# Prompt queries of the second mixer in blocks by residue modulo 4

## The chip, the cores and the metric

The kernel runs as one program on one core of a Trainium2 chip. The metric is the device time of one execution in microseconds. One "layer" of a decoder is computed for 256 prompt tokens and 64 sample tokens (8 sequences of 8), all in float32 accuracy.

## The reference, cut to what matters

The input is projected to queries, keys, values and gates; two attention mixers follow, then a gated merge, a layer norm and an MLP. The second mixer (B) has three groups g of 8 heads. Query t of group g reads the keys t - j*dilation for j = 0..127:

```python
B_PATTERNS = ((128, 1), (512, 4), (2048, 16))     # (window, dilation)
for g, (win, dil) in enumerate(B_PATTERNS):
    o, lse = banded_window_attn(qb[:, :, g, :, None, :], kb[:, :, g], vb[:, :, g], dil)
...
w = jax.nn.softmax(jnp.stack(lses, 0), axis=0)     # the three groups are merged by their softmax sums
o = jnp.sum(w[..., None] * jnp.stack(outs, 0), axis=0)
```

With 256 prompt tokens, dilation 4 lets a query see only keys of its own residue modulo 4, at most 64 of them, and dilation 16 at most 16. The first mixer (A) has 16 query heads on 2 key heads, a window of 128, no dilation, and a sink.

## The kernel before, in words

Activations are held with features on partitions and tokens along the free dimension: 256 prompt tokens and 64 sample tokens, 320 columns. Weights come in chunks of 512 rows by 256 columns (`raw`, a ring of 4). ScalarE rounds a chunk to `whi`, VectorE computes the rest `wlo`, and TensorE multiplies a chunk in 24 matmuls of 320 columns: high by high, high by low, low by high (`chunk`, lines 1202 to 1204). Four chunks make a group of 256 output features in one of two PSUM tensors `psM[0]`, `psM[1]`.

**Projections.** Groups 0 to 3 are A's queries, 4 to 9 B's queries (two per dilation group), 10 A's keys and values, 11 to 16 B's keys, 17 to 22 B's values, 23 to 38 the gates. For queries and keys ScalarE copies swapped halves to `rot` (L532) and VectorE applies the rotation in three instructions (L862, L863, L866), the last one writing `qT` for queries and the staging tile `tT` for keys, and counting up `evac`, which TensorE waits for before it writes that PSUM tensor again two groups later. GpSimd copies B's keys from `tT` to `kTb` (L347). TensorE transposes keys and values (`turn`), and ScalarE copies them out (`turn_out`) and stores them from its own queue to a scratch in DRAM, values also to `vnat` (tokens on partitions, two blocks of 128). `kv_stored` counts the stores. GpSimd waits for all of them, then copies prompt and sample keys and values to the outputs, then loads the cached keys of the first sample sequence.

**Attention under the gates.** The 16 gate groups run as 64 chunks. From group 2 on, the steps of attention are laid between the chunks in an order written out by hand: in each of four rounds j there are 12 units (`UNITS`), unit ("B", e, qb) being head e of pair j in query block qb (128 tokens), for all three dilation groups at once. Per step TensorE issues the scores of the unit two ahead, the values of the one before, and the transposes (turn) of the probabilities of the current one, then a chunk. VectorE scales and masks the scores into `S`, takes the maximum (`front`), later normalizes (`back`); ScalarE computes the exponentials (`exps`) and copies turned probabilities from PSUM to `PT` (`turned_probs`).

A B unit of qb 0 meets keys 0..127 in each group: both heads' scores are issued together, heads alternating, three products of 128 columns each (L1255). A B unit of qb 1 meets 256 keys in each group: each head issues its three products of 256 columns in its own step (L1261). So a unit has 384 or 768 score columns, 3 or 6 turned blocks and, for the pair, 6 or 12 value products (L1314).

Units SB and SA are the samples; their cached keys go to `kvbuf` by GpSimd's loads, new keys are added by GpSimd (`add_new_keys`). At the end the attention output `oT` is split in three parts to `ohi` (ScalarE, L661) and `olo` (VectorE, L960), which the branch projections read.

## Time and profile before

| | |
|---|---|
| median of 3 runs | 1818.94 us (1817.2 to 1819.33) |
| profiled execution | 1818.74 us, span 1817.2 us |
| busy TensorE | 1785.7 us, 98% of the span |
| busy VectorE | 970.0 us, 53% |
| busy ScalarE | 783.7 us, 43% |
| busy GpSimd | 128.9 us, 7% |
| DMA | 369.40 MB, mean 203 GB/s |
| granted TensorE clock | 0.996 of full on the mean |

The span is the time from the first to the last recorded instruction of the profiled execution; the time of that execution is 1.5 us longer. "Busy" is the time in which at least one instruction of the engine is in flight. Matmul records overlap, so the distance between two starts is shorter than the duration of one. A matmul of plain fp32 operands leaves two records, a transpose and a matmul of the split operands one.

### The profile page before, as it was taken

To read this page: it belongs to the slowest core of one execution; us is meant where nothing else is said; L and a number is where in the kernel's file an instruction comes from. 1 tells how busy PE (TensorE), PEld (TensorE's weight loads), DVE (VectorE), ACT (ScalarE), POOL (GpSimd) and SP (SyncE) were. 2 spreads that over 40 slices of the span, in tenths; PEclk is the share of its full clock that TensorE was granted. 3 is DMA by queue.
4 is the path that set the end of the run, shared out by engine and by line. 5 is a ranking of instruction groups with operands and counts; after the bars stand their busy time and mean duration, and the time that the engine had idled before them with its cause. 6 is when DMAs were issued, how large, how long until landed. Compare 5 with 4: busy or idle time off the path is not lost.

```text
span 1817.2 us, 34353 instructions
## 1 busy us (share of the span) xinstructions
PE 1785.7 (98%) x13170; PEld 1753.8 (97%) x13170; DVE 970.0 (53%) x1324; ACT 783.7 (43%) x1109; POOL 128.9 (7%) x251
## 2 busy tenths in 40 slices
PE   7999999999999999999999999999999999999996
PEld 7999999988899899999999999999999999999995
DVE  5555453356665655656767444654446544465465
ACT  5444553455665563334445333443334433344333
POOL 4000000021121110100000000000000000000001
PEclk9999999999999999999999999999999999999998
DMA  8555555587777666655565766657666575656742
GB/s 259 148 150 151 165 169 161 164 316 240 254 244 264 221 240 204 210 163 171 184 208 199 233 222 205 208 187 244 202 224 208 187 245 189 236 187 212 240 149 70
DMA packets 272229, 369.40 MB, mean 203 GB/s; under 512 B 13088, under 2 KB 265952, under 8 KB 269200
## 3 DMA queue, kind: packets, MB, share of 16 engines
q1 hardware_dynamic: 252496, 251.58, 45.0%
q0 software_dynamic: 10368, 107.12, 15.3%
q10 hardware_dynamic: 9280, 9.51, 1.5%
q8 instruction: 61, 1.00, 0.2%
q14 instruction: 24, 0.20, 0.0%
HBM read 356.02 MB, written 70.71 MB: 235 GB/s over the span
## 4 chain that ended last, share of the span: by engine, by line
PE 97%; DMA 1%; DVE 1%; ACT 0%; issue 0%; ACTq 0%; SPq 0%; DVEq 0%
PE psM L1202 30%; PE psM L1203 30%; PE psM L1204 30%; DMA s_raw<-in_w_in_dram 1%; PE psT L1288 1%; PE psM L1276 1%; PE psO L1333 1%; PE psM L1261 1%; PE psO L1314 0%; PE psT L1222 0%; PE psO L1323 0%; PE psM L1265 0%; PE psT L1293 0%; DVE s_r L1186 0%; DMA s_xraw<-in_xT_dram 0%; PE psO L1403 0%
## 5 line engine op out<-in xcount | busy, mean ns | idle before, releaser
L799 DVE TENSOR_TENSOR s_wlo<-s_raw,s_whi 128x1024 fp32r<-128x1024 f32 x468 | 570.0, 1225 | 620.2 <-ACT s_whi L475 615.4
L475 ACT ACTIVATE s_whi<-s_raw 128x1024 fp32r<-128x1024 f32 x468 | 491.2, 1057 | 775.2 <-PE psM L1204 750.0
L1202 PE MATMUL psM<-s_xhi,s_whi 128*128 128x320 f32 x1248 | 392.3, 314 | 9.8 <-DVE s_xlo L804 9.8
L1204 PE MATMUL psM<-s_xhi,s_wlo 128*128 128x320 f32 x1248 | 386.6, 310 | 0.0
L1203 PE MATMUL psM<-s_xlo,s_whi 128*128 128x320 f32 x1248 | 386.6, 310 | 0.0
L1203 PE MATMUL psM<-s_glo,s_whi 128*128 128x322 f32 x1024 | 319.5, 312 | 0.0
L1202 PE MATMUL psM<-s_ghi,s_whi 128*128 128x322 f32 x1024 | 318.7, 311 | 0.0
L1204 PE MATMUL psM<-s_ghi,s_wlo 128*128 128x322 f32 x1024 | 318.5, 311 | 0.0
L1202 PE MATMUL psM<-s_uhi,s_whi 128*128 128x320 f32 x1024 | 316.9, 309 | 0.0
L1204 PE MATMUL psM<-s_uhi,s_wlo 128*128 128x320 f32 x1024 | 316.4, 309 | 0.0
L1203 PE MATMUL psM<-s_ulo,s_whi 128*128 128x320 f32 x1024 | 316.4, 309 | 0.0
L1202 PEld LDWEIGHTS psM<-s_xhi,s_whi 128*128 128x128 f32 x1248 | 235.5, 189 | 10.5 <-DVE s_xlo L804 9.8
L1203 PEld LDWEIGHTS psM<-s_xlo,s_whi 128*128 128x128 f32 x1248 | 235.6, 189 | 0.0
L1204 PEld LDWEIGHTS psM<-s_xhi,s_wlo 128*128 128x128 f32 x1248 | 235.3, 189 | 0.0
L1204 PEld LDWEIGHTS psM<-s_ghi,s_wlo 128*128 128x128 f32 x1024 | 194.1, 190 | 0.0
L1202 PEld LDWEIGHTS psM<-s_ghi,s_whi 128*128 128x128 f32 x1024 | 193.4, 189 | 0.1
L1203 PEld LDWEIGHTS psM<-s_glo,s_whi 128*128 128x128 f32 x1024 | 193.3, 189 | 0.1
L1202 PEld LDWEIGHTS psM<-s_uhi,s_whi 128*128 128x128 f32 x1024 | 192.2, 188 | 0.2
L1203 PEld LDWEIGHTS psM<-s_ulo,s_whi 128*128 128x128 f32 x1024 | 192.2, 188 | 0.2
L1204 PEld LDWEIGHTS psM<-s_uhi,s_wlo 128*128 128x128 f32 x1024 | 192.2, 188 | 0.0
L456 POOL DMA_DIRECT2D out_b_s_dram<-in_cache_b_kv_dram x56 | 27.3, 487 | 763.6 <-DVE s_wlo L799 750.7
L1202 PE MATMUL psM<-s_mhi,s_whi 128*128 128x320 f32 x256 | 79.3, 310 | 0.0
(206 smaller groups left out, 1688.0 us busy)
## 6 DMA issues: line engine op xcount, KB each, us to landing
s_raw<-in_w_ff_dram SPq DMA_DIRECT2D x256, 512.0 KB, 3.9
s_raw<-in_w_in_dram SPq DMA_DIRECT2D x156, 512.0 KB, 4.1
s_kvbuf<-in_kT_b_dram POOLq DMA_DIRECT2D x8, 2448.0 KB, 9.2
s_kvbuf<-in_v_b_dram POOLq DMA_DIRECT2D x8, 2304.0 KB, 8.4
s_raw<-in_w_out_dram SPq DMA_DIRECT2D x32, 512.0 KB, 3.6
out_b_s_dram<-in_cache_b_kv_dram POOLq DMA_DIRECT2D x16, 1008.0 KB, 6.6
s_raw<-in_w_branch_a_dram SPq DMA_DIRECT2D x16, 512.0 KB, 3.6
gates_scratch<-s_gstage ACTq DMA_DIRECT2D x16, 320.0 KB, 3.9
```

The costliest lines, as they stand in the source:

```text
L456: pool.dma_start(dst, src).then_inc(out_cache, 16)
L475: act.activation(whi[:, slot], raw[:, slot], ACT.Copy).then_inc(hi_done, 1)
L799: dve.tensor_tensor(wlo[:, slot], raw[:, slot], whi[:, slot].bitcast(F32), ALU.subtract).then_inc(lo_done, 1)
L1202: pe.matmul(out, wh, xh, start=first and k == 0, stop=False)
L1203: pe.matmul(out, wh, xl, start=False, stop=False)
L1204: mm = pe.matmul(out, wl, xh, start=False, stop=last and k == KT - 1)
L1261: mm = pe.matmul(ps[:, g, 0:nk], qTb[64 * e:64 * e + 64, 4 * g + j, qs], kTb[64 * e:64 * e + 64, 4 * g + j, 0:nk], start=True, stop=True)
L1276: mm = pe.matmul(ps[rows, g, 0:KN], Qz[:, g - 1, c, rows], kcache[:, pr, 4 * g - 3 + c], start=c == 0, stop=c == 3)
L1288: mm = pe.transpose(psTf[:, t * P:t * P + P], Sp[:, t * P:t * P + P], ident[:])
L1333: pe.matmul(out[32 * pr:32 * pr + 16, 0:P], PTz[:, 256 * (g - 1) + 64 * c + 16 * pr:256 * (g - 1) + 64 * c + 16 * pr + 16], vcache[:, 4 * ...
```

## The change

Prompt tokens of B are ordered by residue modulo 4: position r*64 + a holds token 4a + r. A query block of 128 then holds two residues: block 0 residues 0 and 1, block 1 residues 2 and 3.

- Groups of dilation 4 and 16 keep queries (`qT`), keys (`kTb`) and values (`vnat`) in this order, so a query block meets only the 128 keys of its own two residues. Group 0 (dilation 1) has its queries in this order and its keys and values in order of tokens: both of its blocks meet all 256 keys.
- Every B unit has 256 + 128 + 128 = 512 score columns, 4 turned blocks and, for the pair, 8 value products. Both blocks issue the scores of both heads at once.
- Reordering is done by instructions that exist already, each split in two, one for the prompt's columns with a step of four elements on one side and one for the samples' columns: VectorE's last rotation addition for B's queries, GpSimd's copy of keys (groups 13 to 16), ScalarE's copy of values (groups 19 to 22), and the third part of the split of `oT`.
- Values of these groups are stored to the scratch in three DMAs in place of two. `kv_stored` goes to 16 stores per counter.
- The masks become four tables of 256 columns: SP loads the first, GpSimd blanks the others with one memset and fills them by 12 loads.
- In the projections the loop over queries starts two groups later (groups 2 and 3 stand before it) and the loop over values is unrolled.

```diff
-            [("S", [P, 3, 768], F32), ("PT", [P, 2, 768], F32), ...
+            [("S", [P, 3, 512], F32), ("PT", [P, 2, 640], F32), ...
-        mask_p = sb("mask_p", [P, 3, 256])
+        mask_p = sb("mask_p", [P, 4, 256])
...
+        def by_residue(ap):
+            return ap.rearrange("p t (r a) -> p t a r", r=4)
+        def in_order(ap):
+            return ap.rearrange("p t (a r) -> p t a r", r=4)
...
+            nc.gpsimd.memset(mask_p[:, 1:4], NEG).then_inc(masks_blank, 1)
...
+            for r2 in range(2):
+                for h in range(2):
+                    early, late = 64 * r2, 64 * r2 + 32
+                    pool.dma_start(mask_p[early:early + 32, 1 + h, 0:P], rows[:, h, r2, 0, P:2 * P]).then_inc(mask_in, 16)
+                    pool.dma_start(mask_p[late:late + 32, 1 + h], rows[:, h, r2, 0]).then_inc(mask_in, 16)
+                for g in range(2):
+                    first = P * g + 64 * r2
+                    pool.dma_start(mask_p[64 * r2:64 * r2 + 64, 3, first:first + 64], a["mask_p"][0:64, g, P:P + 64]).then_inc(mask_in, 16)
...  # GpSimd, keys of groups 13 to 16
+                    pool.tensor_copy(by_residue(kTb[:, to, 0:SEQ]), in_order(tT[:, c % 2, :, 0:SEQ]))
+                    pool.tensor_copy(kTb[:, to, SEQ:NTOK], tT[:, c % 2, :, SEQ:NTOK]).then_inc(kcopy, 1)
...  # ScalarE, store of values of groups 19 to 22
+                        for r2 in range(2):
+                            act.dma_start(rows[:, :, r2], vnat[64 * r2:64 * r2 + 64, 0:2, bass.ds((g - G_V) * GW + P, GW)]
+                                          ).then_inc(kv_stored[par], 16)
+                        act.dma_start(kvn_d[SEQ:NTOK, bass.ds(dcol, GW)], v_to[1]).then_inc(kv_stored[par], 16)
...  # ScalarE, values of groups 19 to 22 from PSUM
+                        act.activation(by_residue(tT[:, par, :, 0:SEQ]), in_order(ps[:, :, 0:SEQ]), ACT.Copy)
+                        act.activation(tT[:, par, :, SEQ:NTOK], ps[:, :, SEQ:NTOK], ACT.Copy).then_inc(evac[par], 1)
...  # VectorE, B's queries
+                if kind == "qb":
+                    out = qT[:, bass.ds(g * 2, 2)]
+                    dve.tensor_tensor(by_residue(out[:, :, 0:SEQ]), in_order(dst[:, :, 0:SEQ]), in_order(rot[:, :, 0:SEQ]), ALU.add)
+                    dve.tensor_tensor(out[:, :, SEQ:NTOK], dst[:, :, SEQ:NTOK], rot[:, :, SEQ:NTOK], ALU.add).then_inc(evac[par], 1)
...  # VectorE, mask of a B unit
-                    nh, n = 1, 3 * nk
+                    nh, n = 1, 512
+                    last = dve.scalar_tensor_tensor(halves(Sp[:, 0:n]), halves(psM[0][:, e, 0:n]), SCALE, mask_p[:, 1 + qb:4:2 - qb], ALU.mult, ALU.add)
...  # ScalarE, third part of the output's split; VectorE's is split alike
+                act.activation(in_order(ohi[:, 8:12, 0:SEQ]), by_residue(oT[:, 8:12, 0:SEQ]), ACT.Copy)
+                act.activation(ohi[:, 8:12, SEQ:NTOK], oT[:, 8:12, SEQ:NTOK], ACT.Copy).then_inc(o_hi, 1)
...  # TensorE, scores
-                if (kind, e, qb) == ("B", 1, 0):
+                if kind == "B" and e == 1:
                     return
...
-                if kind == "B" and qb == 0:
-                    for g in range(3):
+                if kind == "B":
+                    for g, first, keys in ((0, 0, slice(0, SEQ)), (1, SEQ, qs), (2, SEQ + P, qs)):
                         for h in range(2):
                             half = slice(64 * h, 64 * h + 64)
-                            mm = pe.matmul(psM[0][:, h, P * g:P * g + P], qTb[half, 4 * g + j, qs], kTb[half, 4 * g + j, 0:P], start=True, stop=True)
+                            mm = pe.matmul(psM[0][:, h, first:first + keys.stop - keys.start], qTb[half, 4 * g + j, qs], kTb[half, 4 * g + j, keys],
+                                           start=True, stop=True)
...
-                elif kind == "B":
-                    for g in range(3):
-                        mm = pe.matmul(ps[:, g, 0:nk], qTb[64 * e:64 * e + 64, 4 * g + j, qs],
-                                       kTb[64 * e:64 * e + 64, 4 * g + j, 0:nk], start=True, stop=True)
...  # TensorE, turns and values
-                    for t in range((3 if kind == "B" else 2) * (qb + 1)):
+                    for t in range(4 if kind == "B" else 2 * (qb + 1)):
...
-                    for t in range(nb):
-                        g, kb = divmod(t, qb + 1)
+                    for t, (g, kb) in enumerate(((0, 0), (0, 1), (1, qb), (2, qb))):
```

## Rows read from the trace of the kernel before

**Rows 1.** The page: busy us, share and instructions; the chain that ended last.
```profile
PE 1785.7 (98%) x13170; PEld 1753.8 (97%) x13170; DVE 970.0 (53%) x1324; ACT 783.7 (43%) x1109; POOL 128.9 (7%) x251
...
PE 97%; DMA 1%; DVE 1%; ACT 0%; issue 0%; ACTq 0%; SPq 0%; DVEq 0%
```

**Rows 2.** TensorE's waits, whole span: us in total, times, longest us.
```profile
PE psM L1202 <- DVE s_xlo L804: 9.8, 1, 9.8
PE psT L1288 <- ACT s_PT L569: 2.4, 1, 2.4
```

**Rows 3.** Timeline, TensorE, scores: start us, us of the group, engine, line, count.
```profile
448.52 0.94 PE L1255 MATMUL psM<-s_kTb,s_qT 64*128 64x128 f32 x12
449.39 0.66 PE L1323 MATMUL psO<-s_PT,s_vnat 128*64 128x128 f32 x8
...
411.64 1.56 PE L1261 MATMUL psM<-s_kTb,s_qT 64*128 64x256 f32 x6
413.12 0.66 PE L1323 MATMUL psO<-s_PT,s_vnat 128*64 128x128 f32 x8
...
425.65 0.49 PE L1265 MATMUL psM<-s_kTa,s_qT 64*128 64x128 f32 x4
426.08 0.33 PE L1349 MATMUL psO<-s_ident,s_PT 128*128 128x128 f32 x1
...
431.30 0.70 PE L1265 MATMUL psM<-s_kTa,s_qT 64*128 64x256 f32 x4
431.93 0.87 PE L1288 MATMUL psT<-s_ident,s_S 128*128 128x128 f32 x6
```

**Rows 4.** Timeline, TensorE: a group of turns and two groups of values.
```profile
466.39 0.55 PE L1288 MATMUL psT<-s_ident,s_S 128*128 128x128 f32 x3
...
438.48 1.53 PE L1314 MATMUL psO<-s_PT,s_vnat 128*64 128x128 f32 x24
...
472.62 0.88 PE L1314 MATMUL psO<-s_PT,s_vnat 128*64 128x128 f32 x12
```

**Rows 5.** Groups by line and shape: count, busy us, mean ns, idle before.
```profile
L1288 PE MATMUL psT<-s_ident,s_S 128*128 128x128 f32 x120 | 20.1, 287 | 2.4 <-ACT s_PT L569 2.4
...
L1314 PE MATMUL psO<-s_PT,s_vnat 128*64 128x128 f32 x144 | 9.6, 278 | 0.0
...
L824 DVE COPY s_QbS<-s_qT 64x32 f32<-64x32 f32 x48 | 8.8, 184 | 0.5
```

**Rows 6.** Timeline, ScalarE's and GpSimd's, before the first units; idle before in brackets.
```profile
363.55 0.61 ACTq L494 DMA_DIRECT2D kv_scratch<-s_vst  x1
...
367.09 0.58 POOL L362 DMA_DIRECT2D out_a_p_dram<-kv_scratch  x1 [104.34 <-DMA kv_scratch<-s_vst]
...
394.47 1.06 ACT L475 ACTIVATE s_whi<-s_raw 128x1024 fp32r<-128x1024 f32 x1 [5.33 <-DMA s_raw<-in_w_in_dram]
```

**Rows 7.** Timeline, projections: the last rope instruction, and TensorE's next group.
```profile
202.19 0.82 DVE L866 TENSOR_TENSOR s_tT<-s_tT,s_rot 128x640 f32<-128x640 f32 x1
...
211.55 0.39 PE L1202 MATMUL psM<-s_xhi,s_whi 128*128 128x320 f32 x1
```

**Rows 8.** Instructions of one tile: ns min/median/max, first and last start us.
```profile
L347 POOL COPY s_kTb<-s_tT x6: 718/720/724, 188.3 to 262.0; 128x640 f32 x4, 128x640 f32<-128x640 f32 x2
...
L1202 PE MATMUL psM<-s_ohi,s_whi x192: 309/309/410, 685.6 to 770.8; 128*128 128x320 f32 x192
...
L960 DVE TENSOR_TENSOR s_olo<-s_qT,s_ohi x3: 1484/1485/1492, 674.9 to 677.7; 128x1280 fp32r<-128x1280 f32 x3
```

**Rows 9.** Timeline: GpSimd done with new keys, TensorE's scores of SB; round 0 and tightest.
```profile
433.87 0.54 POOL L382 DMA_DIRECT2D s_vca<-in_cache_a_kv_dram  x1
...
436.25 0.44 PE L1271 MATMUL psM<-s_kvbuf,s_QbS 128*32 128x136 f32 x8
...
540.58 0.54 POOL L382 DMA_DIRECT2D s_vca<-in_cache_a_kv_dram  x1
...
540.78 0.44 PE L1271 MATMUL psM<-s_kvbuf,s_QbS 128*32 128x136 f32 x8
```

More of the change, by code:

```diff
@@ L196, in projections @@
             step(1, 0, 1, "q", None)
-            with eng.Fori(0, 4) as i:
-                for c in range(2, 4):
-                    step(i * 2 + c, i, c, "q", None)
+            step(2, 0, 2, "q", None)
+            step(3, 0, 3, "q", None)
+            with eng.Fori(0, 3) as i:
+                for c in range(4, 6):
+                    step(i * 2 + c, i, c, "qb", None)
             step(10, 0, 10, "kva", None)
@@ L206, in projections @@
             step(17, 0, 17, "v", "k")
-            with eng.Fori(0, 2) as i:
-                for c in range(18, 20):
-                    step(i * 2 + c, i, c, "v", "v")
-            step(22, 0, 22, "v", "v")
+            step(18, 0, 18, "v", "v")
+            step(19, 0, 19, "w", "v")
+            for c in range(20, 23):
+                step(c, 0, c, "w", "w")
+        def by_residue(ap):
+            return ap.rearrange("p t (r a) -> p t a r", r=4)
+        def in_order(ap):
+            return ap.rearrange("p t (a r) -> p t a r", r=4)
         def gate_bank(n):
@@ L341, in _, with kcopy_step @@
                     pool.dma_start(dst[32 * pr + 16:32 * pr + 32, 0:3], a[name][16:32, 0:3]).then_inc(mask_in, 16)
[L343 to L357 removed]
+            pool.wait_ge(masks_blank, 1)
+            rows = a["mask_p"].rearrange("(a h r) g n -> a h r g n", h=2, r=2)
+            for r2 in range(2):
[6 more added lines that the diff above has]
+                    pool.dma_start(mask_p[64 * r2:64 * r2 + 64, 3, first:first + 64], a["mask_p"][0:64, g, P:P + 64]).then_inc(mask_in, 16)
+            def kcopy_step(g, i, c, kind):
+                pool.wait_ge(evac[c % 2], i + (c // 2 + 1))
+                to = bass.ds((g - G_K) * 2, 2)
+                if kind == "k":
+                    pool.tensor_copy(kTb[:, to], tT[:, c % 2]).then_inc(kcopy, 1)
+                else:
+                    pool.tensor_copy(by_residue(kTb[:, to, 0:SEQ]), in_order(tT[:, c % 2, :, 0:SEQ]))
+                    pool.tensor_copy(kTb[:, to, SEQ:NTOK], tT[:, c % 2, :, SEQ:NTOK]).then_inc(kcopy, 1)
+            kcopy_step(11, 0, 11, "k")
+            kcopy_step(12, 0, 12, "k")
+            with pool.Fori(0, 2) as i:
+                for c in range(13, 15):
+                    kcopy_step(i * 2 + c, i, c, "by residue")
+            pool.wait_ge(kv_stored[0], 16 * 16)
+            pool.wait_ge(kv_stored[1], 16 * 16)
             kv_rows = kvn_d.rearrange("t (s c) -> t s c", s=2)
@@ L516, in turn_out @@
                     act.wait_ge(turned_out, g - 9)
-                    store(*v_to, (g - G_V) * GW + (KVW + P), GW)
+                    dcol = (g - G_V) * GW + (KVW + P)
+                    if kind == "v":
+                        store(*v_to, dcol, GW)
+                    else:
+                        rows = kvn_d[0:SEQ, bass.ds(dcol, GW)].rearrange("(a h r) n -> a h r n", h=2, r=2)
+                        for r2 in range(2):
+                            act.dma_start(rows[:, :, r2], vnat[64 * r2:64 * r2 + 64, 0:2, bass.ds((g - G_V) * GW + P, GW)]
+                                          ).then_inc(kv_stored[par], 16)
+                        act.dma_start(kvn_d[SEQ:NTOK, bass.ds(dcol, GW)], v_to[1]).then_inc(kv_stored[par], 16)
             def step(g, i, c, kind, turn):
@@ L890, in front @@
                 if kind == "B":
-                    nh, n = 1, 3 * nk
-                    got = psM[0][:, e, 0:n].rearrange("p (g k) -> p g k", g=3) if qb == 0 else ps[:, 0:3, 0:nk]
-                    last = dve.scalar_tensor_tensor(Sp[:, 0:n].rearrange("p (g k) -> p g k", g=3), got, SCALE, pm, ALU.mult, ALU.add)
+                    nh, n = 1, 512
+                    halves = lambda ap: ap.rearrange("p (g k) -> p g k", g=2)
+                    last = dve.scalar_tensor_tensor(halves(Sp[:, 0:n]), halves(psM[0][:, e, 0:n]), SCALE, mask_p[:, 1 + qb:4:2 - qb], ALU.mult, ALU.add)
                 elif kind == "A":
@@ L896, in front @@
                     for hh in range(2):
-                        last = dve.scalar_tensor_tensor(Sp[:, hh * nk:hh * nk + nk], ps[:, 2 * hh, 0:nk], SCALE, pm[:, 0], ALU.mult, ALU.add)
+                        last = dve.scalar_tensor_tensor(Sp[:, hh * nk:hh * nk + nk], ps[:, 2 * hh, 0:nk], SCALE, mask_p[:, 0, 256 - nk:256], ALU.mult, ALU.add)
                 else:
@@ L957, in end @@
                 split(G_BR - 1, 3)
-                for j in range(3):
+                for j in range(2):
                     dve.wait_ge(o_hi, j + 1)
@@ L1300, in unit_values @@
                     return
-                out, PTk, nb = psO[:, k % 2], PT[:, k % 2], 3 * (qb + 1)
+                out, PTk = psO[:, k % 2], PT[:, k % 2]
                 if kind == "SB":
```

57 lines of the change are left out of this document (28 added, 29 removed).

## The prediction, made before the changed kernel was run

> **What bounds the kernel now.** I read the page's busy shares and its chain of waits first. TensorE is busy 98% of the span and the chain that ended last is 97% TensorE [rows 1]. The share alone does not say that the engine issues without a break, so the next view was the list of what TensorE waited for. It lists a handful of waits, of which two matter: 9.8 us for the first activations, before the change's place, and one wait of 2.4 us in the attention stage [rows 2]. Everywhere else the next instruction issues as soon as the last lets it. So a microsecond of TensorE instructions taken out is a microsecond off the span, as long as no new wait appears, and work on VectorE, ScalarE and GpSimd costs nothing while it stays inside its cover. The price of a TensorE instruction is then the distance from its start to the next start, not its listed duration: durations overlap.
>
> The changed work lies between two chunks of a gate projection, four rounds (j) of 12 units. Four units of a round are the second mixer's prompt units ("B"): two for the first query block (qb 0), two for the second (qb 1).
>
> **TensorE, scores.** Each fp32 product is two matmul records in the trace. qb 0 has three products per head, 128 columns each, heads alternating: 12 records, from 448.52 to 449.39, 0.87 us [rows 3]. qb 1 has three products of 256 columns for one head, then in the next step the same for the other: 6 records, 411.64 to 413.12, 1.48 us, twice a round [rows 3]. That is 0.247 us a record for 256 columns, against 0.0725 for 128 when heads alternate. The other mixer's units show what alternating is worth at 256 columns: its two heads (4 records) take 425.65 to 426.08, 0.43 us, at 128 columns and 431.30 to 431.93, 0.63 us, at 256 [rows 3]. So two heads' 128 extra columns cost 0.20 us. After the change both blocks issue the same pattern: one product of 256 columns and two of 128 for each head, alternating, 12 records. Its price is 0.87 + 0.20 = 1.07 us; I take 1.08. Per round: before 0.87 + 2 x 1.48 = 3.83, after 2 x 1.08 = 2.16, 1.67 less; four rounds **6.7 us**. The new pattern is not in the trace. Its lower end is 0.87 (the extra columns hide behind the weight loads), 1.7 us less over eight issues; its upper end takes the four 256-column records at the lone-head 0.247 and eight at 0.0725, 1.57 us, 3.9 us more over eight. The second mixer's issue differs from the first's only in width, so I stay with 1.08.
>
> The Trainium skill, "TensorE: Matmul & The Clock Gate", Part 3 on packing small matmuls, says that a weight load overlaps a running matmul only when its row group differs. The trace agrees, 0.247 us a record with one head and under 0.16 with two. The same section says that matmuls in different row groups run at the same time, so a pair would cost one; here the rows disagree, and what that would make of the sum is a rival below.
>
> **TensorE, turns and values.** Transposes of probabilities are one record per 128 columns. A group of six lasts 0.87 us and one of three 0.55 [rows 3, 4], so one is 0.107. qb 0 goes from 3 to 4 a unit, qb 1 from 6 to 4: over two units each, two more and four fewer, 0.21 a round, **0.9 us** in all, of 120 records [rows 5] (72 of them B's). Value products: 24 records last 1.53, 12 last 0.88 [rows 4], 0.054 a record. qb 0 goes from 12 to 16 records, qb 1 from 24 to 16: 4 fewer a round, 0.22, **0.9 us**; the 144 records [rows 5] become 128. Ends for these two together: nothing gained (each group's fixed part grows with the new shape), and twice the amount, 3.6.
>
> Sum: 6.7 + 0.9 + 0.9 = 8.5 us. The profiled execution took 1818.74 us, 1817.2 of it span. 1818.74 - 8.5 = 1810.2; the median shown, 1818.94, is 0.2 above that execution, so 1810.4.
>
> **VectorE and ScalarE in the units.** Mask, maximum, exponential, normalization and the copy of turned probabilities go from 384 to 512 columns in qb 0 and from 768 to 512 in qb 1. They lie beside the chunks of the gate projection, TensorE waits for none of them outside the one place below, and the net is less work. I take nothing.
>
> **Projection stage.** The rotated queries of groups 4 to 9 are added into a residue order by two instructions for one, the keys are copied by GpSimd and the values by ScalarE in the same way, with a step of four elements on one side. The last rope instruction starts at 202.19 and takes 0.82; TensorE writes that bank next at 211.55 [rows 7], 8.5 us later. Low end for the strided form: 0.82, as now. High end: the price of the short pieces copied for the samples, 184 ns for 32 elements [rows 5], 5.8 ns an element, 3.7 us for 640. Both are covered; uncovered, the high end would cost 2.9 us in each of the six steps. GpSimd makes its six copies between 188.3 and 262.0 [rows 8], one per 14.7 us group, and ScalarE's copy has the same room. At the end the third split of the attention output (olo) becomes two instructions; the three end at 679.2 and TensorE first reads split outputs at 685.6 [rows 8], the third part two chunks later.
>
> **Queues.** GpSimd gets one memset and 12 small loads more behind 40 of about 0.5 us at the start, some 7 us, so they end near 30 us (an estimate, 52 times 0.5 and the rest), while its next duty is the key copy at 188.3 [rows 8] and VectorE needs the masks only after the projections. SP loads one third of the mask table instead of all. ScalarE issues three stores for two in the last four value steps; the longest such issue took 0.61 us [rows 6]. In the last step it matters: GpSimd waits for those stores until 367.09 [rows 6], then issues the cache outputs and the 2.4 MB of cached keys, which fill the DMA engines. In that crowd a weight load arrives only at 394.47 [rows 6]; ScalarE stands before it, the copy of the first unit's turned probabilities stands behind it, and TensorE's 2.4 us wait [rows 2] is for that copy. A start 0.4 to 0.6 later can lengthen the wait by as much. Against it, 0.3 us of added TensorE work of round 0 (its scores and the first turn) lies before the wait and may be absorbed. I take the two as cancelling; bounds are the wait gone (-2.4) and the wait 3 us longer.
>
> **New keys.** For each SB unit the cached keys are reloaded. In round 0 GpSimd was through with them at 433.87 and TensorE needed them at 436.25 [rows 9], 2.4 us to spare; the two turns between shrink by 0.4. The tightest place is 540.58 against 540.78 [rows 9]; there two first-block turns lie between and the room grows by 0.2. No wait taken.
>
> **Rivals.**
> (a) The crowd clears differently and the 2.4 us wait goes: 1810.4 - 2.4 = 1808.0. For: the wait hangs on one late load. Against: the same bytes move at the same time.
> (b) The wait grows by 1 to 4 us, or a key reload comes late in some rounds: 1811.5 to 1814.5, middle 1812.9. For: the 0.2 us of room [rows 9] and the third store. Against: all intervals that shrink have 2 us left.
> (c) The score issue is not paired in the new mix of widths (upper end above): 1810.4 + 3.9 = 1814.3.
> (d) Matmuls of two heads overlap in time: an issue costs 512 columns in place of 1024, by the 0.20 us that twice 128 columns cost, 0.4 less, eight times 3.3: 1807.1. Against it, 0.63 for 256 columns is 0.43 plus the columns of both heads. The Trainium skill's section named above would give this.
> (e) Slower than before: the store of values in pieces by residue, and the loads behind it, prolong the crowd so that late weights hold TensorE. The place is 367 to 395; the price is one for one from the point where the wait is used up, and it turns the sign when the wait exceeds 2.4 + 8.5 = 10.9 us. At 14 us it would be 1822. For: it is the one spot where TensorE waits today. Against: a crowd of 27 us would have to last 8.5 longer for the same bytes.
>
> The Trainium skill, "SBUF — State Buffer", in its section on the port swizzle, speaks against the change: accesses that cross to a new 16-byte line pay a penalty, and four fp32 elements are such a step. The page gives no size; the trace of before has no such instruction of full width. By the room above, the rope add would have to take 11 times as long before TensorE noticed, so it adds 1 in 100 to (e) and nothing to the sum.
>
> **How the numbers follow.** Forecast 0.76 (its own range 1809.0 to 1811.6); (a) 0.06; (b) 0.08; (c) 0.03; (d) 0.03; (e) with slower mishaps 0.04. Range: 1807.0 to 1813.6 leaves out the upper part of (b), (c) and (e). The measurement cannot tell less than 0.2%, 3.6 us, from no change, so faster is anything under 1815.3. All cases but (e) lie there, save a tail of (b): faster 0.94, same 0.03, slower 0.03.
>
> **What would show it.** On the line of the scores 96 matmul records in eight issues, each near 1.08 us from its start to what follows, none at 1.48; 112 turned blocks in place of 120, 128 value records in place of 144. In TensorE's waits still only the first activations and one wait near 395 of 2 to 3 us. Residue-ordered copies longer or not, without a TensorE wait behind them. Wrong would be: a score issue over 1.3 us, any TensorE wait on key copies (kvbuf) or on rope results, or a wait near 395 far from 2.4 us.

## The result, and the profile after

The changed kernel takes 1806.95 us on the median of four runs (1806.55 to 1807.81), the one before 1818.26 us beside it (four runs, 1817.2 to 1819.33): ratio 0.9938, 95% interval 0.9926 to 0.995, faster. The forecast was 1810.4 us with a range from 1807.0: its sign and its sum of TensorE's instructions hold, the reason it gave for the price of a paired score issue does not, and the time lies 3.4 us below it, just under the range. Unchanged copies of the new kernel were timed twice more: 1808.48 (1805.88 to 1811.28, ratio 0.9946, 0.9933 to 0.996) and 1807.75 us (1806.67 to 1810.39, ratio 0.9947, 0.9934 to 0.9961). The 14 runs of these three sets have the median 1807.5, the 56 runs of the kernel before on the same chips 1817.4 (1816.28 to 1821.69). The change is worth about 9.9 us.

The page of the changed kernel, shares and then the chain, answers to [rows 1]:

```profile
span 1805.0 us, 34241 instructions
...
PE 1775.9 (98%) x13146; PEld 1747.0 (97%) x13146; DVE 971.7 (54%) x1331; ACT 785.5 (44%) x1114; POOL 145.7 (8%) x268
...
PE 97%; DMA 1%; DVE 1%; ACT 0%; issue 0%; ACTq 0%; SPq 0%; DVEq 0%
```

TensorE is still the whole chain, with 24 records fewer: 8 turned blocks and 16 value products, as forecast, and the same 96 score records. The waits of TensorE (us in total, times, longest) answer to [rows 2]:

```profile
PE psM L1252 <- DVE s_xlo L845: 9.8, 1, 9.8
...
PE psT L1335 <- ACT s_PT L608: 0.2, 1, 0.2
```

The wait for turned probabilities is 0.2 us where it was 2.4. The timeline of TensorE after, for [rows 3, 4] (start, us, line, count):

```profile
427.01 0.66 PE L1335 MATMUL psT<-s_ident,s_S 128*128 128x128 f32 x4
...
433.35 1.09 PE L1360 MATMUL psO<-s_PT,s_vnat 128*64 128x128 f32 x16
434.37 0.44 PE L1335 MATMUL psT<-s_ident,s_S 128*128 128x128 f32 x2
...
442.98 1.15 PE L1305 MATMUL psM<-s_kTb,s_qT 64*128 64x256 f32 x12
444.05 0.67 PE L1369 MATMUL psO<-s_PT,s_vnat 128*64 128x128 f32 x8
```

A score issue takes 442.98 to 444.05, 1.07 us, and the other seven take 1.08; sixteen value products take 1.02 from their start to the next group's, four turns last 0.66. The groups by line and shape (count, busy us, mean ns, idle before), for [rows 5, 7, 8]:

```profile
L1335 PE MATMUL psT<-s_ident,s_S 128*128 128x128 f32 x112 | 19.3, 289 | 0.2 <-ACT s_PT L608 0.2
...
L1360 PE MATMUL psO<-s_PT,s_vnat 128*64 128x128 f32 x128 | 8.8, 279 | 0.0
...
L909 DVE TENSOR_TENSOR s_qT<-s_tT,s_rot 128x512 f32 x6 | 6.6, 1094 | 1.4 <-DVE s_rot L904 1.4
...
L373 POOL COPY s_kTb<-s_tT 128x512 f32 x4 | 4.5, 1131 | 51.7 <-DVE s_tT L912 51.7
L579 ACT ACTIVATE s_tT<-psM 128x512 f32<-128x512 f32 x4 | 4.4, 1109 | 0.0
...
L701 ACT ACTIVATE s_ohi<-s_qT 128x1024 fp32r<-128x1024 f32 x1 | 2.1, 2106 | 0.0
```

The reordering instructions cost 1.7 to 2.1 times as much per element as the plain ones, and no TensorE wait stands behind them. Their order of access is not the step of four elements that the section on the change speaks of: the residue runs fastest (the destination of L579 counts 4, then 64), so on the reordered side four elements in turn lie 64 elements (256 bytes) apart, and the other side is read or written in order.

**Where the time is.** The starts of the chunks' matmuls cut the span into stages (us). "First 98" runs from the start of the first matmul to the start of the 98th, a little over four chunks; "to first scores" from there to the last chunk matmul ahead of the first scores; the attention stage from that one to the last chunk matmul ahead of the last unit's values, which take another 1.0 on both sides. The clock is taken to have risen at the first matmul that starts less than 0.2 us ahead of the next.

| kernel, execution | first matmul | first 98 | to first scores | attention | its wait | branch gap | clock rises at |
|---|---|---|---|---|---|---|---|
| before, first profile | 9.79 | 16.98 | 353.21 | 290.47 | 2.4 | 0.53 | 15.8 |
| after, first profile | 9.81 | 15.82 | 353.21 | 279.93 | 0.2 | 0.16 | 13.2 |

The two spans differ by 12.2 us. The attention stage gives 10.5, of which 2.2 are the wait and 8.3 instructions; the start gives 1.2, the branch projections 0.5 (a gap of 0.53 us ahead of their fourth chunk where 0.15 is usual, and 0.1 behind it). Everything else agrees within 0.02 us. The start is a matter of the clock. The timeline of the kernel before, and then of the one after:

```profile
15.56 0.37 PE L1202 MATMUL psM<-s_xhi,s_whi 128*128 128x320 f32 x1
15.77 0.31 PE L1203 MATMUL psM<-s_xlo,s_whi 128*128 128x320 f32 x1
```

```profile
12.91 0.42 PE L1254 MATMUL psM<-s_xhi,s_wlo 128*128 128x320 f32 x1
13.16 0.31 PE L1252 MATMUL psM<-s_xhi,s_whi 128*128 128x320 f32 x1
```

TensorE was idle to 9.8 us, starts at half clock (1.2 GHz, matmuls 0.27 us apart) and reaches 2.4 GHz (0.15 apart) at 15.8 in the one and 13.2 in the other. Three questions were open: whether the start and the wait are the change's doing or the execution's, what makes the gap, and whether pairing is what makes the score issue cheap.

### The profile page after: what moved, and what is told of

It reads as the page before. It is cut to its first block, busy times and chain, and to the rows that moved or that the text cites. A ratio compares the mean times of both kernels' runs of the same rounds, so it can differ in the third digit from the quotient of the medians.

```text
span 1805.0 us, 34241 instructions
## 1 busy us (share of the span) xinstructions
PE 1775.9 (98%) x13146; PEld 1747.0 (97%) x13146; DVE 971.7 (54%) x1331; ACT 785.5 (44%) x1114; POOL 145.7 (8%) x268
## 3 DMA queue, kind: packets, MB, share of 16 engines
q0 software_dynamic: 10752, 107.38, 15.3%
## 4 chain that ended last, share of the span: by engine, by line
PE 97%; DMA 1%; DVE 1%; ACT 0%; issue 0%; ACTq 0%; SPq 0%; DVEq 0%
PE psM L1252 30%; PE psM L1253 30%; PE psM L1254 30%; PE psT L1335 1%; DMA s_raw<-in_w_in_dram 1%; PE psM L1323 1%; PE psO L1379 1%; PE psT L1272 0%; PE psO L1360 0%; PE psO L1369 0%; PE psM L1305 0%; PE psM L1312 0%; PE psT L1340 0%; DVE s_r L1236 0%; DMA s_xraw<-in_xT_dram 0%; PE psO L1449 0%
```

## The experiments

**Repeats of both kernels, profiled.** `before_again` and `after_again` are the kernels unchanged.

> The kernel before, unchanged, profiled once more. Open is how much of the 12.2 us between the two profiled spans belongs to the execution and not to the change. Theory 1: the moment at which TensorE's matmuls go from 0.267 us apart to 0.147 apart (15.6 us in the first profile of before, 13.2 in that of after) and the 2.4 us wait for the turned probabilities both vary from one execution to the next; here either differs from the first profile by over 0.3 us. Theory 2: both belong to the kernel: again 15.6 us and a wait of 2.2 to 2.6 us.

> The changed kernel, profiled and timed once more. Both theories: the eight score issues take 1.08 us each again, the issue terms give 8.4 us. Theory 1 (clock rise and wait vary by execution): the rise lies anywhere between 12 and 16 us, the wait near 391 anywhere between 0 and 2.5 us, and the timed difference to before lies between 8.4 and 12. Theory 2 (the change makes the rise earlier and removes the wait): rise at 13.2 and wait 0.2 again, timed difference 11 to 12.

before_again took 1817.87 us, after_again's profiled execution 1811.28. TensorE's wait in before_again, and in after_again with the stretch behind it (busy us of TensorE, its weight loads, VectorE, ScalarE, GpSimd, then granted clock, DMA share, GB/s):

```profile
PE psT L1288 <- ACT s_PT L569: 1.4, 1, 1.4
```

```profile
PE psT L1335 <- ACT s_PT L608: 2.9, 1, 2.9
```

```profile
397.50:400.50 3.00, 3.00 (x13) 3.00 (x12) 2.41 (x10) 2.29 (x7) 0.00 (x0) 0.50 0.65 191
```

The wait differs between executions of the same program, 2.9 here against 0.2; and after 2.9 us of waiting the clock falls to 0.50 for twelve chunk matmuls, 1.4 us more. Less the wait and this, the stage is 279.6 us, as in the first profile (279.7), and that of before_again is 288.4 (288.0 in the first), 0.2 of it a second wait, for the new keys of a sample unit at 610.3. So the instructions are constant, and 0.2 us is not what the changed kernel always waits; whether its mean wait is shorter is asked again at the end of the experiments.

**The pairing alone.** `own_step` gives each head its scores in its own step, as block 1 had them before; `head_by_head` issues both heads in one step, but one after the other.

```diff
-                if kind == "B" and e == 1:
-                    return
...
-                        for h in range(2):
+                        for h in (e,):
```

> The changed kernel, but each head issues its own three score products in its own step, not both heads alternating. Theory (a weight load into the rows that are in use is not hidden: 0.247 us for 256 columns is 0.107 of columns and 0.14 of load): 6 records are 2 x 0.247 + 4 x 0.19 = 1.26 us, a pair of steps 2.5 against 1.08, so 1.44 us more eight times, 11.5 us slower than the changed kernel, about no gain left over before. Rival (only wide lone products are dear, 128 columns cost 0.073 anyhow): 0.78 us a step, 3.9 us slower than the changed kernel. Rival (alternation is worth nothing, columns count): the same as the changed kernel within 1 us.

```diff
-                    for g, first, keys in (...):
-                        for h in range(2):
+                    for h in range(2):
+                        for g, first, keys in (...):
```

> The changed kernel with both heads' scores in one step, but all three products of one head before those of the other. If the alternation of heads is what makes an issue cheap, it costs about what own_step costs: an issue near 2.4 us, 10 to 11 us slower than the changed kernel. If having both heads in one step is what counts (one entry into plain fp32 work instead of two), it stays near 1.1 us an issue and within 1 us of the changed kernel.

own_step takes 1815.72 us (10 runs, 1814.95 to 1816.64; ratio to the kernel before 0.9989, 0.998 to 0.9999), head_by_head 1810.62 (5 runs, 1810.28 to 1811.16; 0.9964, 0.9951 to 0.9977). Timelines of own_step and then of head_by_head:

```profile
446.39 1.14 PE L1303 MATMUL psM<-s_kTb,s_qT 64*128 64x256 f32 x6
447.46 0.67 PE L1367 MATMUL psO<-s_PT,s_vnat 128*64 128x128 f32 x8
```

```profile
443.79 1.68 PE L1305 MATMUL psM<-s_kTb,s_qT 64*128 64x256 f32 x12
445.41 0.67 PE L1369 MATMUL psO<-s_PT,s_vnat 128*64 128x128 f32 x8
```

One head's six records alone take 1.07 us, as long as both heads' twelve when they alternate. Sixteen such issues against eight: 8.5 us, and the stage less its wait is 288.6 against 279.7. Without the pairing the change keeps 1.4 us against the runs of the kernel before beside it (1.7 against all 56), of its 9.9. So most of the gain is not fewer score columns but that block 1 can be paired at all: `psM[0]` has 1024 columns, two heads of 512 fit into it, two of 768 did not.

Why a pair costs no more than one head is seen when the views are cut off before the third record of a pair, or the second of a lone head, starts. TensorE in the kernel before (block 0, heads alternating), in the changed kernel and in own_step:

```profile
448.52 0.38 PE L1255 MATMUL psM<-s_kTb,s_qT 64*128 64x128 f32 x2
```

```profile
442.98 0.49 PE L1305 MATMUL psM<-s_kTb,s_qT 64*128 64x256 f32 x2
```

```profile
446.39 0.48 PE L1303 MATMUL psM<-s_kTb,s_qT 64*128 64x256 f32 x1
```

With alternating heads two records start within 0.007 us of each other, one of each head, and both have the listed duration of a lone one (0.48, two together 0.49). The next two follow when the next record of a lone head would: six pairs take 1.076 us, six lone records 1.070. The matmuls of the two heads run at the same time. A record that has its rows to itself, or a pair, costs 0.216 us at 256 columns and 0.11 at 128; each issue has some 0.2 us more at its two ends.

head_by_head shows the same at its change of heads. TensorE up to 444.333 and up to 444.340:

```profile
443.79 0.81 PE L1305 MATMUL psM<-s_kTb,s_qT 64*128 64x256 f32 x3
```

```profile
443.79 1.02 PE L1305 MATMUL psM<-s_kTb,s_qT 64*128 64x256 f32 x4
```

The first head has six records, and the fourth record to start, 6 ns behind its third, is the second head's first, of 256 columns (a duration of 0.48). It runs beside the rest of the first head. An issue takes 1.61 us: 0.54 more than alternating, eight times 4.3, and the stage grew by 4.1. Two lone issues would be 2.14; 0.32 of the difference is that one record running beside the others, 0.2 the ends paid once. Neither expectation is met: it costs neither what own_step costs nor what alternation costs.

The 11.5 us expected of own_step came from a weight load that a lone head cannot hide. The same load stands before records of both widths, and the 128 columns more cost 0.105 us, nearly all of the 0.11 that a lone record of 128 costs: columns set the price, and no room is left for a constant load of 0.14. The Trainium skill, "TensorE: Matmul & The Clock Gate", Part 3, says that matmuls in different row groups run concurrently, starting some 4 ns apart; the trace agrees, with 6 to 7 ns.

**Start and crowd removed on both sides.** In `before_warm_late` and `after_warm_late` TensorE multiplies constants into an unused PSUM tile before the first activations, and GpSimd's copies to the cache outputs are issued behind the last load of cached values (at 640 us), not ahead of the cached keys. `after_out_late` has the second edit alone.

```diff
+            pe.wait_ge(zeroed, 1)
+            for _ in range(WARM):      # 14
+                pe.matmul(psO[:, 0, 0:P], onesD[:], onesD[:], start=True, stop=True)
...  # GpSimd: the loop of the output copies moved from before load_k to after the last load_v
```

> The kernel before with two additions that take the two varying parts out: 14 plain fp32 matmuls of a constant tile while TensorE waits for the first activations, and the copies of new keys and values to the outputs issued after the last load of cached values instead of before the first load of cached keys. Profiles so far: the first 320-column matmuls are 0.267 us apart for 2.5 to 5.9 us, which costs 1.2 to 2.6 us, and the wait for turned probabilities is 2.4 and 1.4 us in two profiles. Theory: neither is left, so 3 to 5 us less than before, and repeated times closer together than 1 us. Rival: the clock falls back in the gap to the first real matmul, or the wait is made by the 2.4 MB load of keys alone: then under 2 us less.

> The same two additions to the changed kernel. Theory (the change is worth its TensorE issue time and nothing else): 8.4 us less than before_warm_late, within 0.5. Rival (the change also takes away wait or clock time for good): the difference stays at the 10 to 11 us of the plain pair. Against the changed kernel itself 2 to 5 us less, so the fastest of the four.

> The changed kernel, only the copies of new keys and values to the outputs issued later. Profiles of the changed kernel: wait 0.2 us in one; 2.9 us in the other, and behind it 12 matmuls 0.267 us apart that cost 1.4 more, spans 4.7 us apart. Theory: this wait is what scatters its times (1805.9 to 1811.3); without it they lie within 2 us of each other (what the clock's rise leaves) near the lower end, 1805.5 to 1807. Rival: the scatter is from elsewhere and stays 4 to 5 us.

before_warm_late takes 1815.2 us (10 runs, 1814.97 to 1816.5; ratio 0.9988, 0.9979 to 0.9997), after_warm_late 1805.95 (5 runs, 1805.88 to 1806.37; 0.9933, 0.9919 to 0.9946): the lowest median here on both sides of the change. The changed kernel's five times lie within 0.5 us of each other, where its three unchanged sets had 1.3, 5.4 and 3.7; those of before_warm_late lie within 1.5, not 1. Against the kernel as it was the two edits give 2.2 us before and 1.6 after, less than the 3 to 5 and the 2 to 5 expected. First scores and first chunk after the units, of before_warm_late and then of after_warm_late:

```profile
379.20 0.94 PE L1259 MATMUL psM<-s_kTb,s_qT 64*128 64x128 f32 x12
...
667.91 0.41 PE L1202 MATMUL psM<-s_xhi,s_whi 128*128 128x320 f32 x1
```

```profile
378.83 1.15 PE L1309 MATMUL psM<-s_kTb,s_qT 64*128 64x256 f32 x12
...
659.07 0.41 PE L1252 MATMUL psM<-s_xhi,s_whi 128*128 128x320 f32 x1
```

288.71 against 280.24 us, 8.47 apart, with no wait for probabilities on either side. This is the change's instructions by themselves, and the forecast sum of them was 8.5. The pair's medians differ by 9.25, above the 8.4 within 0.5 that was expected and below the rival's 10 to 11: 8.47, 0.47 in the branch stage, and some 0.3 at the start (0.4 in the two profiled executions).

after_out_late takes 1808.34 us (1806.97 to 1808.81; 0.9943, 0.9929 to 0.9956), not the 1805.5 to 1807 expected of it, though its times lie within 1.8 us of each other as expected: in its profile the wait for probabilities is gone, but one of 1.5 us stands in another place, behind a weight load that arrived 4.8 us late at 382.58.

```profile
PE psM L1251 <- ACT s_gstage L656: 1.5, 1, 1.5
```

Moving the copies takes the crowd's tail away, not the load of 2.4 MB, so a late weight chunk is still a matter of the execution. The constants did less than their name says, too. TensorE of before_warm_late at the start (idle before in brackets):

```profile
1.28 6.28 PE L1240 MATMUL psO<-s_onesD 128*128 128x128 f32 x28 [1.28 <-POOL s_onesD L335]
9.73 0.42 PE L1202 MATMUL psM<-s_xhi,s_whi 128*128 128x320 f32 x1 [2.17 <-DVE s_xlo L804]
...
10.90 0.47 PE L1203 MATMUL psM<-s_xlo,s_whi 128*128 128x320 f32 x1
```

The real matmuls start at full spacing, fall back to half clock (listed at 0.47 us) at 10.9, behind the gap of 2.2 us, and rise again at 14.1. `after_warm19_late` has 19 of them in place of 14.

> after_warm_late with 19 in place of 14 constant matmuls at the start. With 14 they ended near 7.5 us, the first real matmul came at 9.5, ran 0.147 apart until 10.8 and then 12 matmuls at 0.267: the 2 us gap was followed by a fall of the clock. Theory (idle time ahead of the first chunk is what the clock falls for): with the gap filled to under 0.6 us no matmul of the first chunk is 0.267 apart, 1.5 us less than after_warm_late, near 1804.4. Rival (constant matmuls do not hold the clock up, or the fall comes anyway): the same 12 slow matmuls, 1805.9.

Its gap is still 1.9 us, since each of the later ones takes half as long, yet no real matmul is slow; the first 98 matmuls take 0.33 us less and no more, because gaps of 0.2 to 0.4 us now stand ahead of the second, third and fourth chunk (at 13.5, 17.6 and 21.4), one of them a wait of 0.26 for activations: the engines that feed TensorE bound it there. 1806.11 us (1805.7 to 1808.03; 0.9937, 0.9924 to 0.9951), no better than 14.

**The reordering alone.** `reorder_only` has the changed kernel's reordered data, its mask loads and stores by residue, and before's units: block sizes, scores, turns and values. The amount of work in the units is that of the kernel before.

> The changed kernel with the attention units of before: queries, keys, values, masks, stores and the last split in the new order and form, but each query block of B meets the keys of before in the order of before. It leaves out what makes the masks fit the new order. Theory (the reordering is fully covered): the time of before within 1 us, scores at 0.87 and 1.48 us an issue, no TensorE wait behind a reordering copy. Rival (strided copies or the third store cost TensorE something): slower than before by over 1 us, with a wait on evac, kcopy or kv_stored in the projections. Rival (reordering itself gives something, an earlier or later crowd): faster than before by over 1 us.

1816.54 us (11 runs, 1814.83 to 1821.14; ratio 0.9992, 0.9983 to 1.0001). Its attention stage less its waits is 288.1 us, as before the change. Its waits in that stage:

```profile
PE psT L1347 <- ACT s_PT L616: 2.0, 1, 2.0
...
PE psM L1330 <- DVE s_QaS L879: 0.7, 2, 0.3
```

No wait in the projections stands behind a reordering copy: all of the reordering is hidden. The branch gap is gone here as well, so it isn't the units that removed it. `before_split_end` makes one edit to the kernel before: the third part of the output's split in two instructions, without any reordering.

```diff
+                act.activation(ohi[:, 8:12, 0:SEQ], oT[:, 8:12, 0:SEQ], ACT.Copy)
+                act.activation(ohi[:, 8:12, SEQ:NTOK], oT[:, 8:12, SEQ:NTOK], ACT.Copy).then_inc(o_hi, 1)
...  # and olo on VectorE alike
```

> The kernel before, only the third part of the split of the attention output made by two instructions for one on ScalarE and on VectorE, without the new order. In all profiles of before the fourth branch chunk starts 0.53 us after the matmul ahead of it, in all of the changed kernel 0.16, and VectorE's third weight split of that stage starts 0.49 us after ScalarE's against 0.12. Theory (the added instructions shift where VectorE's and ScalarE's programs stand at that place): gap 0.16 here too. Rival (it belongs to another part of the change): 0.53 as before. Either way the time is that of before within 1 us.

1817.09 us (10 runs, 1816.34 to 1818.38; 0.9995, 0.9986 to 1.0005). The fourth chunk of the branch, in the first profile of before and then here:

```profile
696.04 0.31 PE L1204 MATMUL psM<-s_ohi,s_wlo 128*128 128x320 f32 x1
696.57 0.41 PE L1202 MATMUL psM<-s_ohi,s_whi 128*128 128x320 f32 x1 [0.22 <-issue]
```

```profile
695.49 0.31 PE L1210 MATMUL psM<-s_ohi,s_wlo 128*128 128x320 f32 x1
695.66 0.41 PE L1208 MATMUL psM<-s_ohi,s_whi 128*128 128x320 f32 x1
```

The gap of 0.53 us is 0.17 with the added instructions and no others, and TensorE's last matmul comes 0.45 us sooner after the units; the median is too close to that of before to show it. Its releaser is "issue", so nothing that the profile shows held TensorE. VectorE's weight split ahead of it is late by as much, 0.37 us: in before it starts 0.49 us behind the end of ScalarE's rounding of that chunk (at 694.41), here 0.12 (at 693.50). What delays both, and why two more instructions on other engines remove it, stays open.

**How much room the projections have.** The strided addition 7 times in a row per group (`again` orders them):

```diff
-                    dve.tensor_tensor(by_residue(out[:, :, 0:SEQ]), ...)
+                    for r in range(7):
+                        if r > 0:
+                            dve.wait_ge(again, g * 7 + (r - 28))
+                        dve.tensor_tensor(by_residue(out[:, :, 0:SEQ]), ...).then_inc(again, 1)
```

> The changed kernel, with VectorE's strided addition of B's queries made seven times in place of once, each waiting for the one before: some 1.1 us each, 6 to 7 us more per group of queries, six groups. Theory (8 us of room between the rotation and TensorE's next use of the bank): no TensorE wait in the projections, the last matmul before the first scores at the same distance from the first chunk as ever, 353.2 us behind the 98th. Rival (the room is smaller, since VectorE's weight splits queue behind): a TensorE wait on VectorE of over 1 us in six places and 6 us or more longer.

One run, 1814.26 us. TensorE's waits, and VectorE's timeline:

```profile
PE psM L1256 <- DVE s_wlo L841: 2.9, 3, 1.1
PE psT L1339 <- ACT s_PT L609: 2.5, 1, 2.5
```

```profile
87.80 7.96 DVE L913 TENSOR_TENSOR s_qT<-s_tT,s_rot 128x512 f32 x7 [0.23 <-DVE s_rot L905]
95.58 0.30 DVE L914 TENSOR_TENSOR s_qT<-s_tT,s_rot 128x128 f32 x1
95.79 4.62 DVE L841 TENSOR_TENSOR s_wlo<-s_raw,s_whi 128x1024 fp32r<-128x1024 f32 x4
```

Six additions of 1.14 us, 6.8 in all, make the projections 4.2 us longer over six groups, with three TensorE waits of 1.1 us at most: between the two expectations. What is late is the split of the next weights behind them on VectorE: its first ends at 97.0, while TensorE's last matmul started at 95.7. So the room is about 5.5 us, not the 8.5 to the bank's next use that I had read, and it ends at a different instruction. The change uses 0.56 of it. The 2.5 us wait for probabilities and six matmuls at half clock behind it make up much of the rest of this run's time.

**More draws of start and wait.** `after_third` and, one after the other on one chip, `before_clock1`, `after_clock1`, `before_clock2`, `after_clock2` are unchanged copies, run to see whether the early rise of the clock goes with the changed kernel.

> The changed kernel a third time. Attention from the last matmul before the first scores to the same matmul after the units took 279.9 us in its first profile with a wait of 0.2, 283.9 in the second with a wait of 2.9 and 12 slow matmuls. Theory (wait and clock differ by execution): taken out, 279.6 to 279.8 again, whatever the span is; the median of all its timings settles 9 to 10.5 us under that of before. Rival (the changed kernel as a rule has no wait): a wait under 0.5 us.

> The kernel before, for the moment at which its first matmuls go from 0.267 to 0.147 us apart. If the moment belongs to the kernel: 15.3 to 15.6 us as in three profiles. If it is the execution's: anywhere between 12.4 and 15.6, so that a value under 15 appears in one of this and the next.

> The changed kernel, the same question. If the earlier rise belongs to the changed kernel: under 15 us again (12.9, 14.9, 12.4 so far). If it is the execution's: 15.3 to 15.6 appears in one of this and the next, as it did in after_out_late. The attention stage less waits and slow matmuls is 279.5 to 279.7 us in either case.

> The kernel before once more, the same question and the same two expectations: 15.3 to 15.6 us if the rise belongs to the kernel, anywhere from 12.4 if to the execution.

> The changed kernel once more, the same question and the same two expectations: under 15 us if the early rise belongs to the changed kernel, 15.3 to 15.6 in this or the last if to the execution.

| execution | us | clock rises at | wait for probabilities | attention less waits |
|---|---|---|---|---|
| before / again | 1818.74 / 1817.87 | 15.8 / 15.6 | 2.4 / 1.4 | 288.0 / 288.3 |
| before_clock1 / 2 | 1817.94 / 1818.66 | 14.8 / 15.2 | 1.6 / 2.1 | 288.3 / 288.1 |
| after / again | 1806.55 / 1811.28 | 13.2 / 14.9 | 0.2 / 2.9 (and 1.4 at half clock) | 279.7 / 279.6 |
| after_third | 1807.30 | 12.7 | 1.4 | 279.5 |
| after_clock1 / 2 | 1807.19 / 1808.46 | 15.3 / 16.3 | 0.0 / 0.8 | 279.5 / 279.5 |

Each number is from the execution's own timeline and waits; the last column has all waits of the stage taken out, in before_again and before_clock2 also one of 0.2 and 0.3 at a sample unit near 610 us, which no profile of the changed kernel has. The expectations read the rise up to 0.3 us earlier in some profiles. It ranges over 14.8 to 15.8 before and 12.7 to 16.3 after: an early rise isn't a property of the changed kernel. The wait lies at 1.4 to 2.4 before, 1.9 on the mean, and at 0 to 2.9 after, 1.1 on the mean. Four and five draws don't tell whether its mean moved; they do tell that it is drawn anew each time.

What is drawn is when one weight load lands. In every profile with this wait the copy of the turned probabilities starts 0.96 us behind the start of ScalarE's rounding of one and the same weight chunk, which came late: ScalarE had idled for it 4.3 to 5.3 us in the four profiles of before, 3.0 to 5.6 in four of after. In after_clock1 that chunk was in time, and the load that came late, by 4.0 us, was the next one:

```profile
397.04 1.06 ACT L502 ACTIVATE s_whi<-s_raw 128x1024 fp32r<-128x1024 f32 x1 [4.02 <-DMA s_raw<-in_w_in_dram]
```

The copy stood ahead of it, and TensorE did not wait. The change does move the crowd: its last store is issued 0.8 us later against the first scores in every profile that stores by residue (15.9 us ahead of them in place of 16.7), and GpSimd's first copy starts 11.1 to 12.2 us ahead of them in the five profiles of after, 13.0 to 13.1 in the four of before. Whether that shortens the wait on the mean is not shown; reorder_only has the later crowd too, and a wait of 2.0.

## Why the prediction missed its time, point by point

- **The place that bounds, and the sum.** Right. TensorE is the chain, a microsecond of its instructions is one off the span, and 8.5 us were forecast for them; the pair without waits shows 8.47. That the three terms come out one by one is shown by the starts in the trace: scores 6.8, turns 0.86, values 0.85.
- **Scores, 6.7.** Right in size, wrong in mechanism. An issue takes 1.07 to 1.08 in all eight, at the value I took between 0.87 and 1.57, and own_step shows that the alternation makes it. But I had the heads' columns run one after the other, at 0.20 us for twice 128, with alternation only hiding the weight loads. The records of the two heads run at the same time, and a column costs a pair what it costs a lone head, some 0.8 ns (0.105 us for 128), where 0.20 us for 512 columns one after the other is 0.4 ns. Half as many columns in turn at twice the price come to the same 0.20, so the sum could not tell the two apart, and that it came out right was luck. I also wrote that the rows disagree with concurrent matmuls; the first two records of [rows 3] start 0.007 us apart, and they agree.
- **Turns and values, 0.9 each.** Right: 112 and 128 records. Four turns last 0.66 where six lasted 0.87, 0.105 a record; sixteen values last 1.09 where twelve lasted 0.88 and twenty-four 1.53, 0.054 a record.
- **VectorE, ScalarE, stores, masks, key reloads.** Right to take nothing: no wait on any of them, and reorder_only is not slower than the kernel before. I took the crowd to start 0.4 to 0.6 us later, which was too little: the last store is issued 0.8 later, and the crowd starts 0.8 to 2.0 later. Its price in time cannot be told from the draws.
- **Room for the strided addition.** Wrong in size and place, without effect: 5.5 us, not 8.5, ahead of the weight split. I looked for who needs the instruction's output and not for who queues behind it. The Trainium skill, "SBUF — State Buffer", port swizzle section, has a penalty for each access that crosses to a new 16-byte line; the trace agrees, and gives 1094 + 283 ns for 826, far from the 5.8 ns an element of my upper end.
- **The step that failed is what stands outside the sum: the execution that it was subtracted from.** I kept the 2.4 us wait whole ("I take the two as cancelling"), and I took the start of that execution as fixed without saying so. Both are draws. The profiled execution before had the longest wait and the latest rise of its kernel's four here; the median of three shown, 1818.94, is 1.5 us above the median of 56. The two profiles then put a high draw of before against a low draw of after: of the 12.2 us between them, 8.3 are instructions, 2.2 the wait, 1.2 the start and 0.5 the branch gap. I allowed 2.4 down for the wait and nothing for the start, where start and wait together move a time by some 2 to 3 us either way. Of the 3.45 us by which 1806.95 lies under 1810.4, 1.5 are the base, 0.5 is the branch gap, 0.6 is that these four runs lie below the median of 14, and 0.9 is left (rounded).
- **The branch gap, 0.47.** Missing from the sum. The row that shows it stood in the trace of before, as a wait of 0.2 us on "issue"; nothing in the profile said that the edit there would remove it.
- **Rivals.** Rival (a), the wait gone, is what the first profile of after shows, but not as a rule of the changed kernel, whose five profiles have 0 to 2.9: 1808.0 for it, less 0.5 for the gap and 1.2 for the start, is 1806.3, and 1806.55 was measured. (b), a wait grown by 1 to 4 us, is near what after_again's profile shows, 0.5 more and 1.4 at half clock, on the same grounds. (c) falls by the 1.07 us issue, (e) by every run. Of (d) the price falls, 0.67 an issue, and the mechanism holds: the heads do overlap, but they did so already in the 0.87 us issue from which I took off another 0.4, so there was nothing more to gain.

From the 1817.4 us of 56 runs, 8.5 and 0.5 less is 1808.4, 0.9 above what 14 runs of the changed kernel give. In the profiles the mean wait is 0.8 shorter and the 98th matmul starts 0.4 sooner on the mean after the change; that would cover it, but so few draws that scatter by 1 us and more don't show it, and it stays open.

## What to carry to other kernels

When TensorE is the chain, the sum of its instructions can be forecast to a tenth of a microsecond from the distances between starts, and pairing two heads of 64 rows is worth half of their issue: one of them is free. A price that fits the rows does not prove the picture behind it; look at the starts of single records, not only at groups. The rest of the error is in the base: before subtracting, ask of every wait and every stretch at half clock in the profiled execution whether another execution would have it, and put its whole size on both sides of the range. For the room of an instruction look at what queues behind it on its own engine, before who reads its result.

## What the runs showed of the hardware

- A wait of 2.9 us was followed by twelve matmuls at a granted clock of 0.50, one of 2.5 (rope_more) by six; waits of 2.4 and less at the same place by none in any profile. After idling to between 9.6 and 10.1 us the rise to 2.4 GHz came anywhere from 12.7 to 16.3 us in the nine profiles of the two kernels.
- Two plain fp32 records on different 64 rows start 6 to 7 ns apart and run at the same time; a pair takes as long as one record alone, 0.216 us at 256 columns and 0.11 at 128. Each score issue has some 0.2 us more at its ends: 1.07 us for six lone records (four of 128, two of 256), 1.08 for six pairs.
- Four fp32 elements in turn that lie 256 bytes apart, on one side: VectorE 2.1 ns an element (1094 ns for 512) against 1.3 (826 for 640), ScalarE 2.06 (2106 for 1024) against 0.99 (1263 for 1280), GpSimd 2.2 (1131 for 512) against 1.1 (720 for 640).
- In the crowd of cached keys and output copies between 367 and 395 us (DMA share 0.99 in the first profile of before) ScalarE idled for a weight load 5.3 us in that profile, 3.0 in the first of after (splitting the chunk at 391.23 in place of 394.47), 4.8 in after_out_late and not at all in after_warm_late.
